# Grouped attention heads on 64 and 65 rows without pads, and the rounded w_out in other tiles, half of it made during the output projection

## The reference

```python
def attend(q, keys, vals, scale):
    s = jnp.einsum('bqhgd,bkhd->bhgqk', q, keys) * scale
    p = jax.nn.softmax(s.astype(jnp.float32), axis=-1).astype(vals.dtype)
    return jnp.einsum('bhgqk,bkhe->bqhge', p, vals)
...
q = rms_norm(q.reshape(bsz, t, GQA_HEADS, HEAD_DIM), q_norm_w)      # HEAD_DIM = 64
k = rms_norm(k.reshape(bsz, t, GQA_KV_HEADS, HEAD_DIM), k_norm_w)
...
x = x + gate[:, None, :] * (jnp.concatenate([y_a, y_b, y_c], axis=-1) @ w_out[l])
if want_ctx:      # layer 0 only
    ctx = ctx + gate_c * (jnp.concatenate([yc_a, yc_b, yc_c], axis=-1) @ w_out[l])
```

## Time and profile before

| | |
|---|---|
| median of 3 runs | 1058.33 us (1055.46 to 1059.82) |
| profiled execution, its own time | 1060.43 us |
| its span, first to last instruction | 1058.5 us |
| mean granted TensorE clock | 0.965 of full speed |
| PE busy | 965.3 us, 91% of the span, 4563 matmul records |
| PEld busy | 669.5 us, 63% |
| DVE busy | 504.3 us, 48% |
| ACT busy | 419.8 us, 40% |
| POOL busy | 136.2 us, 13% |

### The profile page before, as it was taken

The page is one execution under the profiler, slowest core; times in us unless marked ns, Lnnn a source line. Parts: engine busy times, 40 slices in busy tenths (PEclk is TensorE's granted clock), DMA queues, the critical chain, the costliest instruction groups (busy, mean ns, idle before and its releaser), DMA issues.

```text
span 1058.5 us, 12485 instructions
## 1 busy us (share of the span) xinstructions
PE 965.3 (91%) x4563; PEld 669.5 (63%) x4563; DVE 504.3 (48%) x857; ACT 419.8 (40%) x750; POOL 136.2 (13%) x156
## 2 busy tenths in 40 slices
PE   1679999999899999999899969999998999999896
PEld 0368889888555554455568758789774545445475
DVE  0356334433674444554543276434548445555443
ACT  3435234321212445566760255333321244555802
POOL 3000000000243001000361010000003300100620
PEclk9889999999898999999999979999998899999999
DMA  9902121320400223122034102130413000022021
GB/s 334 279 21 60 24 77 40 80 61 2 159 1 1 80 80 102 57 79 81 1 139 97 72 20 68 52 97 4 120 32 148 1 1 1 0 80 80 1 100 79
DMA packets 71962, 74.36 MB, mean 70 GB/s; under 512 B 8196, under 2 KB 51552, under 8 KB 71776
## 3 DMA queue, kind: packets, MB, share of 16 engines
q1 hardware_dynamic: 67888, 60.81, 18.5%
q0 software_dynamic: 4016, 12.77, 3.4%
HBM read 69.37 MB, written 4.19 MB: 70 GB/s over the span
## 4 chain that ended last, share of the span: by engine, by line
PE 81%; DVE 7%; issue 3%; ACT 3%; DMA 3%; POOL 1%; SPq 1%; ACTq 0%; DVEq 0%; POOLq 0%
PE pv L1563 10%; PE bank L1395 9%; PE bank L1396 9%; PE bank L1397 9%; PE bank L1614 5%; PE bank L1524 3%; PE bank L1645 3%; PE bank L1646 3%; PE bank L1647 3%; DMA W<-in_w_mod 3%; PE bank L1491 2%; PE bank L1471 2%; PE bank L1540 2%; PE bank L1340 2%; PE bank L1383 2%
## 5 line engine op out<-in xcount | busy, mean ns | idle before, releaser
L1395 PE MATMUL bank<-hA_parts,W_parts 128*128 128x512 f32 (+1 forms) x496 | 181.1, 365 | 15.1 <-DVE W_parts L945 15.1
L1396 PE MATMUL bank<-hA_parts,W_parts 128*128 128x512 f32 (+1 forms) x496 | 175.2, 353 | 0.0
L827 ACT ACTIVATE hA<-bank 128x512 f32<-128x512 f32 (+1 forms) x168 | 92.6, 561 | 82.0 <-PE bank L1614 56.1
L1194 DVE TENSOR_REDUCE mxp<-bank 128x1 f32<-128x384 f32 x192 | 96.5, 550 | 47.3 <-PE bank L1524 47.0
L1395 PEld LDWEIGHTS bank<-hA_parts,W_parts 128*128 128x128 f32 x496 | 96.4, 194 | 31.5 <-DVE W_parts L945 15.6
L1397 PE MATMUL bank<-h_low_parts,W_parts 128*128 128x512 f32 (+1 forms) x310 | 109.9, 354 | 0.0
L1396 PEld LDWEIGHTS bank<-hA_parts,W_parts 128*128 128x128 f32 x496 | 96.3, 194 | 13.6 <-issue 2.4
L1563 PE MATMUL pv<-hA,vg 128*128 128x512 f32 (+1 forms) x168 | 83.0, 576 | 6.9 <-ACT hA L827 6.4
L1563 PE MATMUL pv<-hA,XA 128*128 128x512 f32 (+1 forms) x168 | 81.0, 563 | 2.4 <-ACT hA L827 2.3
L945 DVE TENSOR_TENSOR W_parts<-W,W_parts 128x1024 fp32r<-128x1024 f32 x44 | 53.4, 1222 | 35.7 <-ACT W_parts L597 35.6
L1212 DVE SCALAR_TENSOR_TENSOR hA<-pv,hA 64x512 f32<-64x512 f32 (+1 forms) x36 | 21.6, 599 | 91.8 <-ACT hA L770 91.6
(11 more groups left out here) (236 smaller groups left out, 1827.2 us busy)
## 6 DMA issues: line engine op xcount, KB each, us to landing
W<-in_w_mod SPq DMA_DIRECT2D x12, 2048.0 KB, 8.1
W<-in_w_in SPq DMA_DIRECT2D x42, 512.0 KB, 4.0
W<-in_w_out SPq DMA_DIRECT2D x4, 2048.0 KB, 7.9
XA<-in_x SPq DMA_DIRECT2D x4, 512.0 KB, 10.0
XA<-in_x POOLq DMA_DIRECT2D x4, 512.0 KB, 7.0
x_between_layers<-XA POOLq DMA_DIRECT2D x4, 512.0 KB, 2.9
XA<-x_between_layers POOLq DMA_DIRECT2D x4, 512.0 KB, 4.8
out<-XA POOLq DMA_DIRECT2D x4, 512.0 KB, 2.9
```

What stands on the lines that cost most here:

```text
L827: act.activation(prob[slot % 4][:, 0:nq], ps("sc", l, h, q0, kt)[:, 0:nq], ACT.Exp, scale=MLA_SCALE if h < MLA_H else GQA_SCALE)\
L1194: dve.tensor_reduce(mxp[:, t, half:half + 1], ps("mx", l, h, q0, t, half)[:, 0:384], AX, ALU.max).then_inc(*up("part_max", l, h, q0, t, half))
L1395: pe.matmul(p[:, 0:c[1]], high[:, k, :], h_hi[:, k, toks], start=(k == 0), stop=False)
L1396: pe.matmul(p[:, 0:c[1]], low[:, k, :], h_hi[:, k, toks], start=False, stop=False)
```

## The change

Two things are changed. First, the grouped heads lose their pads: the row of maxima and ones goes to row 64, straight below the 64 dimensions, the second score matmul takes 65 rows in place of 97, and the maxima matmul 64 rows in place of 96. `k_low` moves from the upper parts of the `wuq` and `wukv` tiles to slices of `h_low`, and POOL writes the ones there right after `head_ones(2)`, in front of the rounding of head 1's keys; its six pad instructions go, and so do the waits for them. Second, the tiles of `w_hi` are dealt out anew: n = 0 gets tiles that are free once the linear attention is done (`glav`, `glaqk`, `sq`), n = 1 gets `gqk` and `rounded`. The pieces of n = 0 are made one at a time at eight units of heads 8 to 10, listed in `W_HIGH_AT` (in layer 0 the unit counted is j - 2), those of n = 1 all at once behind the last `y_hi`. POOL's subtractions follow in the same order.

```diff
+W_HIGH_AT = [(8, 5), (9, 1), (9, 2), (9, 3), (9, 4), (10, 1), (10, 2), (10, 3)]
...
-        k_twice, k_low = ([e[:].rearrange("p f h c -> p (f h c)")[:, o * T:(o + 1) * T]
-                           for e in (wuq_parts, wukv_parts)] for o in range(2))
+        k_twice = [e[:].rearrange("p f h c -> p (f h c)")[:, 0:T] for e in (wuq_parts, wukv_parts)]
+        k_low = [h_low[:, 1 + g, :] for g in range(2)]
...
-        w_hi = [pieces(gqk_parts[:].rearrange("p f t -> p (f t)"), glav_parts[:].rearrange("p t c -> p (t c)")),
-                pieces(rounded[:].rearrange("p f t -> p (f t)"), glaqk_parts[:].rearrange("p f t -> p (f t)"),
-                       sq_parts[:].rearrange("p a b -> p (a b)"))]
+        w_hi = [pieces(glav_parts[:].rearrange("p t c -> p (t c)"), glaqk_parts[:].rearrange("p f t -> p (f t)"),
+                       sq_parts[:].rearrange("p a b -> p (a b)")),
+                pieces(gqk_parts[:].rearrange("p f t -> p (f t)"), rounded[:].rearrange("p f t -> p (f t)"))]
...
                 head_ones(2)
+                for g in range(2):
+                    if g:
+                        pool.wait_ge(*at("k_one", l, 0))
+                    pool.memset(k_low[g][64:65, :].bitcast(F32), 1.0).then_inc(*up("k_one", l, g))
+                pool.wait_ge(*at("k_one", l, 1))
...
-                    pool.memset(k_low[g][64:96, :].bitcast(F32), 0.0).then_inc(*up("k_pad", l, g, 0))
-                    pool.memset(k_low[g][96:97, :].bitcast(F32), 1.0).then_inc(*up("k_pad", l, g, 1))
-                pool.wait_ge(*at("k_pad", l, 1, 1))
-                for b in range(2):
-                    pool.wait_ge(*at("filled", "sc", l, MLA_H + b - 2, 256, TILES - 1))
-                    pool.memset(q_high[b][64:96, :].bitcast(F32), 0.0).then_inc(*up("q_pad", l, b))
-                pool.wait_ge(*at("q_pad", l, 1))
...
                         if n == 0:
-
+                            act.wait_ge(*at("filled", "o", l, TILES - 1))
+                            act.wait_ge(*at("y_gla", l, TILES - 1))
+                        else:
                             act.wait_ge(*at("q_both", l, heads[-1]))
                             act.wait_ge(*at("k_low", l, 1))
                             act.wait_ge(*at("q_low", l, heads[-1]))
-                            act.wait_ge(*at("filled", "o", l, TILES - 1))
-                        else:
-                            act.wait_ge(*at("k_low", l, 1))
-                            act.wait_ge(*at("q_low", l, heads[-1]))
-                            act.wait_ge(*at("y_gla", l, TILES - 1))
...
-                        queries = (qh if h < MLA_H else q_high)[h % 2]
-                        act.activation(queries[96:97, q0:q0 + nq], ps("nm", l, h, q0)[0:1, 0:nq], ACT.Copy)\
+                        queries = qh[h % 2][96:97, :] if h < MLA_H else q_high[h % 2][64:65, :]
+                        act.activation(queries[:, q0:q0 + nq], ps("nm", l, h, q0)[0:1, 0:nq], ACT.Copy)\
...
-                        c = j - 3 if h == heads[-2] else j + len(todo) - 4 if h == heads[-1] and j else -1
-                        if 0 <= c < KD:
-                            w_high(2 * c // KD, (2 * c % KD, 2 * c % KD + 1))
+                        u = j - len(todo) + TILES
+                        if h in (8, 9, 10) and (h, u) in W_HIGH_AT:
+                            w_high(0, (W_HIGH_AT.index((h, u)),))
...
                 y_high((6, 7))
+                w_high(1, range(KD))
...
-                            pe.wait_ge(*at("q_pad", l, h % 2))
-                            q, k = q_high[h % 2][0:96, :], k_twice[(h - MLA_H) // 3][0:96, :]
+                            q, k = q_high[h % 2][0:64, :], k_twice[(h - MLA_H) // 3][0:64, :]
...
-                            mm = pe.matmul(p[:, 0:nq], k_low[g][0:97, keys], q_high[h % 2][0:97, queries],
+                            mm = pe.matmul(p[:, 0:nq], k_low[g][0:65, keys], q_high[h % 2][0:65, queries],
```

More of the change, by code:

```diff
@@ L1609, in _ @@
                                 pe.wait_ge(*at("k_low", l, (h - MLA_H) // 3))
-                                pe.wait_ge(*at("k_pad", l, 1, 1))
+                                pe.wait_ge(*at("k_one", l, 1))
                         p = open_("sc", l, h, q0, kt)
```

## The result

The changed kernel takes 1075.1 us, the median of four runs (1068.67 to 1078.59); the kernel before took 1059.07 beside it (four runs, 1055.46 to 1060.13). The ratio is 1.0144, 95% interval 1.0092 to 1.0195: slower by 16 us. Six more runs of the same kernel came later; over all ten the median is 1072.3, and they fall in two groups: six from 1068.7 to 1072.7, four from 1078.4 to 1078.9. What makes two groups of one kernel is a part of the story.

The account below looks back on a forecast made before the run. TensorE (PE), full in grouped units, was taken to bound the kernel. On 1058.33 us, +16.2 for 64-row maxima and -6.6 for w_out, the rest 0, gave 1067.9; likeliest case 1063 to 1072, outer range 1052.5 to 1074.

Parts of the forecast that it names:

- The maxima on 64 rows: Grouped heads 6 to 11: 54 maxima pairs leave TensorE's whole-array shape, 18.3 us together, net +16.2.
- the upper bound: Grouped heads: each 64-row maxima pair pays 0.38 us, as 32-row matmuls do; the lower bound was 0.
- the net term: Grouped heads, both layers: 18.3 us for 64-row maxima less 2.1 of bank waits that go, +16.2 us.
- The absorbed part: Heads 6, 9, 10 and layer 1: slower PE finds DVE less late, so bank waits go, -2.1 us.
- 65-row scores, pads and ones: Grouped heads' scores and POOL's queue: 65 rows act as 97, removed pads and earlier ones delay nothing, 0 us.
- The w_out part: Heads 9 to 11 and layer 1's output projection: redealt ACT roundings shorten PE's waits, -6.6 us.
- The late half and the reload: Output projection: second-half w_out ready 6 us early in layer 1, later reload of x delays nothing, 0 us.
- (a): Rival, grouped heads: 64-row maxima cost nothing, only -6.6 stays, 1051.7 us; chance 0.22.
- (b): Rival, grouped heads: idle of ACT and DVE hides half the shape switch, 1060 us, no change; chance 0.12.
- (c): Rival, heads 9 and 11: the switch costs and little is won from w_out, 1073 us; chance 0.14.
- (d): Rival, layer 0's projection: reload of x too late for the banks, 1072 us and more; chance 0.03.
- The step that failed: Grouped-head units of 1.67 us: PE has no slack, so whatever is added to a unit is added to the kernel.

Follow-up runs that it names:

- e2: Changed kernel with the old dealing and timing of the rounded w_out, so the heads' part alone: 1081.49 us, ratio 1.0213 to the kernel before.
- e9: Changed kernel, unchanged, run again with a second profile: 1072.16 us, ratio 1.014 to the kernel before.
- e1: Kernel before with only the new dealing and timing of the rounded w_out: 1052.01 us, ratio 0.9927.
- e5: Changed kernel with each pair of 64-row maxima matmuls split around the value pair, doubling the shape changes: 1103.27 us, ratio 1.0413 to the kernel before.
- e3: Kernel before with one line edited, grouped maxima matmuls on 64 rows in place of 96: 1081.05 us, ratio 1.0199.
- e4: Changed kernel with maxima on 96 rows again, using zero-filled rows, 65-row scores kept: 1049.98 us, ratio 0.9913 to the kernel before.
- e6: Changed kernel with zero-filled 96-row maxima, each pair split around the value pair: 1053.31 us, ratio 0.9939 to the kernel before.
- e8: Kernel before with the new dealing of the rounded w_out and grouped keys rounded early by POOL: 1045.98 us, ratio 0.9869.
- e7: Changed kernel, 64-row maxima kept, with POOL rounding grouped keys early and ACT's key copies moved later: 1064.87 us, ratio 1.0054 to the kernel before.

## Why the prediction was right in direction and 7 us short

Times of heads between maxima turns, from the profiled executions, with falls where they were (e2 for head 5 and e9 for the others give layer 0 without a fall):

```
                       before   e1      after, no fall   e1 to after
layer 0, heads 5-8     63.4     63.4    69.3             +5.9
layer 0, heads 9, 10   30.1     29.1    30.6             +1.5
layer 1, heads 5-10    76.3     77.1    83.0             +5.9
last turn to last projection matmul, layer 1
                       58.6     53.2    53.3              0
```

*The maxima on 64 rows.* The choice of the upper bound, 0.38 a pair, was right: 0.40 in the unit, 0.38 for the further excursion of e5's unit. It was read from 32-row and narrow 64-row matmuls, and holds for 64 rows by 128 columns. This is in line with the Trainium skill, TensorEngine Tiling (Array Packing), cited there: by its section Key Properties changing the tiling mode drains the array, and the modes under Available Configurations have 64 x 128 and none of 96. The page gives no time, and the time shown here is 0.4 us for going out and back; that it is a drain, no row shows. Over all heads the net term measures 7.4 + 5.9 = 13.3 us where the forecast had 16.2. The absorbed part was under-sized: in head 6 of layer 1, 12.07 before and 12.46 after, its four pairs cost 0.4 together, as PE waited there anyway (0.61, 0.25 and at the turn 0.28 in e1, one wait of 0.23 after).

*65-row scores, pads and ones: 0.* Shown by e3 against e2, and by the 1.68 of e4's unit.

*The w_out part: -6.6, measured -6.5 (e1).* Its terms were less even than their sum. Heads 9 and 10 of layer 0 gave 1.0 (forecast 0.5), head 11 of layer 0 2.4 (2.0; from the turn to the projection 13.62 before, 11.24 in e1), the end of layer 1, head 11 and projection, 5.4 (4.1), and heads 5 to 10 of layer 1 lost 0.8, where I had nothing. These make -8.0 between the two profiled executions, which differ by 8.5.

*The late half and the reload: 0.* The projection of the kernel after runs without a wait in both layers (555.66 to 621.13, which is 288 matmuls at 0.227; 1022.87 to 1066.50), and the 6 us to spare came out as 6.

*Rivals.* (a), rows cost nothing, falls with the unit of 2.07. (b), half hidden, falls with 13.3. (c) gives nearly the right time, but for another reason: the w_out part won all it was to win. (d) did not happen.

*The step that failed* is the sum itself: "In these units PE has no slack, and whatever is added to a unit is added to the kernel" prices every unit at the full clock, and the sum has no term for the clock. What the traces add up to, against the profiled execution of before (1060.43), with the shape's cost and the w_out part as measured above:

```
                                  after        e9 (the same kernel)
shape, at the full clock         +13.3        +13.3
w_out part                        -8.0         -8.0
fall in head 5, layer 0           +3.2         +3.2
fall in head 6, layer 0           +7.6            0
outside the heads                 +1.7         +1.2
sum                              +17.8         +9.7
measured                         +17.9         +9.8
```

The fall in head 5 is 21.84 and 21.82 against 18.61 in e2. The line outside the heads is the time to the first turn and the time from layer 0's projection to the first turn of layer 1. In the eleven profiles these vary from 327.1 to 332.2 us and from 295.2 to 301.0, in no order of the changes, so a single profile says nothing of 1 or 2 us there. So the two terms of the forecast make +5.3 where it had +9.6, and the falls, put at nothing, make 3.2 to 10.8. That the time came as near as 7 us was luck in part: terms 4 us too dear stood in for falls that were left out. The median of all ten runs, 1072.3, would owe it to the same luck that it lies inside the outer range. The two groups of the ten runs stand 8 us apart, as these two columns do, though only two of the ten have a trace.

The kernel of e3 has the old w_out and is counted from before: its shape costs 14.6 at the full clock (by e2, 5.9, 2.0 and 6.7 in the first three rows of the table of heads), its falls 3.2 in head 5, 3.1 and 1.5 in heads 10 and 11, and 1.7 in head 5 of layer 1, and outside the heads it is 3.6 shorter: 20.5, measured 1081.11 - 1060.43 = 20.7. For e2, without falls, it is 14.6 + 0.3, measured 14.9.

*What decides whether the clock falls* is shown in part. Of the six profiles with 64-row maxima five have a fall inside the heads, nine falls in all; of the five with 96 rows (before, e1, e4, e6, e8) one has one, short. Each of the ten falls came behind waits of PE of 0.8 to 2.6 us (the shortest in e7, the longest in e5) in front of units with maxima, and taking the waits of heads 5 and 6 away or down (e7) took the falls there away in the profiled execution. But the same wait with 64 rows can pass (e2, e9 in head 6), the wait with 96 rows can be followed by one (e4), and a wait of 2.10 us before was not the earlier trace rows. So falls came mostly where waits and changes of shape stood together. That the two together make them likely is argued from eleven profiles and not shown; neither one nor both brought a fall every time, and why one execution has it and the next not stays open.

## What to carry to other kernels

Fewer rows in a matmul save no time, but from 96 to 64 rows the matmul leaves the shape of its neighbours, at 0.4 us for going out and back: in a stream of whole-array matmuls keep such ones above 64 rows with zeros, or put them side by side so that the change is paid once. Where the trace shows PE full, price an added stall twice, once at the full clock and once with the stretch behind the nearest wait at half of it, and make the range reach there. Copies that stand in ACT's queue in front of an exponential for which PE waits are worth moving: e1 moved the roundings of w_out, with POOL's subtractions behind them, and won 6.5 us, e8 those of the keys too and won 6 more.

## What the runs showed of the hardware that was not expected

- The clock fell to 1.2 GHz behind waits of only 1.2 to 1.5 us, and stayed there for 7 and for 17 us in which PE had no wait at all; these stretches cost 3.2 and 7.6 us.
- One kernel, on one chip, takes 1069 to 1073 or 1078 to 1079 us; between its two profiled executions, 1070.22 and 1078.37, one of these stretches is the difference. Four runs were not enough to place its median: 1075.1 by the first four, 1072.3 by ten.
- The price of a change of shape is the same, 0.38 to 0.40 us out and back, for 32-row and 64-row matmuls, and 65, 96 and 97 rows pay nothing. At the lower clock it hardly grows: the unit of 3.79 us holds work of 2 x 1.67 = 3.34 (an estimate from the unit of before), which leaves 0.45.
